# Four banks for the branch tiles, two weight differences made earlier and a residual loaded later, at the end of a two-block fp32 kernel

## What is computed

```python
merged = (jax.nn.sigmoid(m_a + b_merge[l, 0]) * (o_a @ w_branch_mla[l])
          + jax.nn.sigmoid(m_b + b_merge[l, 1]) * (o_b @ w_branch_dsa[l]))
x = x + merged @ w_out[l]
```

## Time and profile before

| | |
|---|---|
| median of 3 runs | 1223.42 us (1223.24 to 1223.59) |
| the profiled execution, whole | 1223.16 us |
| its span, first to last instruction | 1221.4 us |
| TensorE busy (matmuls) | 1208.3 us, 99% of the span |
| VectorE busy | 810.6 us, 66% |
| ScalarE busy | 645.6 us, 53% |
| HBM read and written | 109 GB/s over the span |

### The profile page before, as it was taken

One profiled execution on the slowest core, in us unless ns is written; L12 is line 12 of the kernel. 1 busy time (PEld: TensorE's weight loads), 2 busy tenths in 40 slices (PEclk: granted clock), 3 DMA queues, 4 the chain that ended last, 5 costly groups with the idle time before them and its releaser, 6 DMA issues.

```text
span 1221.4 us, 15497 instructions
## 1 busy us (share of the span) xinstructions
PE 1208.3 (99%) x5796; PEld 984.7 (81%) x5796; DVE 810.6 (66%) x1244; ACT 645.6 (53%) x930; POOL 72.8 (6%) x149
## 2 busy tenths in 40 slices
PE   8999999999999999999999999999999999999998
PEld 7888888888888888888888888888877777777876
DVE  7736543783565366559378475598679989656798
ACT  7645544663554463544444362465566555566732
POOL 2101110210111021000000000000000000000000
PEclk9999999999999999999999999999999999999999
DMA  6421322323132235313215224115213333635711
GB/s 214 136 88 36 112 69 77 103 77 103 43 112 69 78 104 203 127 35 130 112 35 189 86 65 176 35 52 207 78 60 122 118 128 109 227 119 181 276 35 69
DMA packets 25623, 134.22 MB, mean 110 GB/s; under 512 B 3352, under 2 KB 3528, under 8 KB 12768
## 3 DMA queue, kind: packets, MB, share of 16 engines
q1 hardware_dynamic: 16224, 107.14, 25.5%
q0 software_dynamic: 4736, 16.90, 4.0%
q10 hardware_dynamic: 4608, 9.44, 2.0%
HBM read 121.92 MB, written 11.55 MB: 109 GB/s over the span
## 4 chain that ended last, share of the span: by engine, by line
PE 89%; DVE 8%; issue 1%; ACT 1%; DMA 0%; ACTq 0%; DVEq 0%
PE proj L327 60%; PE proj L2015 7%; PE pm L2015 3%; PE pa L2015 3%; PE pm L1920 2%; PE pa L1931 1%; PE pa L2210 1%; PE pa L1892 1%; DVE w_lo L300 1%; PE pm L1902 1%; DVE idx L1568 1%; PE proj L1941 1%; PE pa L1941 1%; PE proj L2253 1%; PE pa L2190 1%
## 5 line engine op out<-in xcount | busy, mean ns | idle before, releaser
L327 PE MATMUL proj<-h_hi,w_hi 128*128 128x512 f32 (+1 forms) x840 | 328.7, 391 | 0.0
L327 PE MATMUL proj<-h_hi,w_lo 128*128 128x512 f32 (+1 forms) x840 | 323.9, 386 | 0.0
L327 PE MATMUL proj<-h_lo,w_hi 128*128 128x512 f32 (+1 forms) x840 | 323.6, 385 | 0.0
L300 DVE TENSOR_TENSOR w_lo<-w_raw,w_hi 128x2048 fp32r<-128x2048 f32 x80 | 182.5, 2289 | 51.7 <-ACT w_hi L294 51.3
L294 ACT ACTIVATE w_hi<-w_raw 128x2048 fp32r<-128x2048 f32 x80 | 152.4, 1913 | 68.6 <-PE proj L2015 44.2
L327 PEld LDWEIGHTS proj<-h_hi,w_hi 128*128 128x128 f32 x840 | 157.8, 188 | 35.6 <-issue 5.0
L327 PEld LDWEIGHTS proj<-h_hi,w_lo 128*128 128x128 f32 x840 | 157.8, 188 | 31.9
L327 PEld LDWEIGHTS proj<-h_lo,w_hi 128*128 128x128 f32 x840 | 158.0, 188 | 31.3 <-issue 1.0
L327 PE MATMUL proj<-w_hi,h_hi 128*128 128x512 f32 (+1 forms) x224 | 87.8, 392 | 0.4 <-issue 0.4
L327 PE MATMUL proj<-w_hi,h_lo 128*128 128x512 f32 (+1 forms) x224 | 86.8, 387 | 0.0
L327 PE MATMUL proj<-w_lo,h_hi 128*128 128x512 f32 (+1 forms) x224 | 86.7, 387 | 0.0
(11 more groups left out here) (499 smaller groups left out, 2244.2 us busy)
## 6 DMA issues: line engine op xcount, KB each, us to landing
w_raw<-in_wall SPq DMA_DIRECT2D x91, 1024.0 KB, 5.1
b<-in_wall SPq DMA_DIRECT2D x9, 1024.0 KB, 7.0
gates<-gate_st ACTq DMA_DIRECT2D x24, 256.0 KB, 2.0
m_all<-gates POOLq DMA_DIRECT2D x2, 1280.0 KB, 6.8
x_res<-in_x ACTq DMA_DIRECT2D x4, 512.0 KB, 4.9
bc<-gate_rows POOLq DMA_DIRECT2D x8, 256.0 KB, 3.5
x_res<-in_x POOLq DMA_DIRECT2D x4, 512.0 KB, 4.4
x<-x_res POOLq DMA_DIRECT2D x2, 1024.0 KB, 4.5
```

What stands on the lines that cost most here:

```text
L300: nc.vector.tensor_tensor(w_lo[:, slot, 4 * half:4 * half + 4, :], w_raw[:, half], w_hi[:, slot, 4 * half:4 * half + 4, :], ALU.subtract)\
L327: mm = nc.tensor.matmul(proj[:, bank, 0:cols] if tokens else proj[:, bank, toks], lhsT, rhs, start=(k == 0 and q == 0), stop=(k == kts - 1 ...
```

## The change

The branch tiles go in turn to four banks instead of two: `proj[:, 0]`, `proj[:, 1]`, and the two banks of `FIN_W`. Tile j waits for the product of tile j - 4 instead of j - 2. The third product of the last projection, which writes `FIN_W`, now waits for the product of tile 15, a wait that stood ahead of the fifth. The two weight differences are made ahead of the products of tiles 6 and 7 instead of 9 and 11; the first goes to a new buffer `f_three`, which lies where `f_hi`'s slots 2 and 3 are, so ScalarE waits for its low part before it writes slot 2. The two low parts of weights stand one tile earlier. POOL loads the residual only when `b12` and `b21` have landed.

```diff
+        f_three = at("f_three", -24 * K, [P, 4, 512])
...
+        BRANCH = (proj[:, 0], proj[:, 1], RES[2], RES[3])
...
             if not first:
-                nc.tensor.wait_ge(S["tile_free"], n - 1)
+                nc.tensor.wait_ge(S["tile_free"], n - 1 if free is None else free)
+            out = proj[:, bank] if out is None else out
...
             gp.wait_ge(S["o_sb"], 8)
+            gp.wait_ge(S["b12_landed"], 16 * CHUNKS + 16)
+            gp.wait_ge(S["w_landed1"], 16 * G_FIN)
             gp.dma_start(x_fin[:, :, :], x2_d.rearrange("(t p) d -> p t d", p=P)).then_inc(S["x2_landed"], 16)
...
-            fin_weight(1, 1, w_sum[:, 1, 4:8])
+            fin_weight(1, 1, f_three[:, :, :])
...
             a.wait_ge(S["merged"], 8)
+            a.wait_ge(S["d_lo"], 7 * CHUNKS + 2)
             fin_operand(2, f12)
...
             for j in range(2 * KT):
                 n = T_BR + j
-                if j == KT + 1:
+                if j == 6:
                     v.wait_ge(S["w_landed1"], 16 * G_FIN)
                     v.wait_ge(S["b12_landed"], 16 * CHUNKS + 16)
-                    v.tensor_tensor(w_sum[:, 1, 4:8], b21, b12[:, :, :], ALU.subtract).then_inc(S["t_made"], 1)
-                if j == KT + 3:
-                    fin_weight(1, 0, b11, 1)
+                    v.tensor_tensor(f_three[:, :, :], b21, b12[:, :, :], ALU.subtract).then_inc(S["t_made"], 1)
+                if j == 7:
+                    v.wait_ge(S["w_landed0"], 16 * G_FIN)
                     v.wait_ge(S["t_made"], 4 * CHUNKS + 1)
                     v.tensor_tensor(b12[:, :, :], b12[:, :, :], b11, ALU.subtract).then_inc(S["t_made"], 1)
-                if j == KT + 5:
-                    fin_weight(1, 1, w_sum[:, 1, 4:8], 2)
+                if j == KT + 2:
+                    fin_weight(1, 0, b11, 1)
+                if j == KT + 4:
+                    fin_weight(1, 1, f_three[:, :, :], 2)
                 v.wait_ge(S["tile_free"], n)
                 v.wait_ge(S["tile_made"], n + 1)
                 v.wait_ge(S["m_sig"], j + 1)
-                v.tensor_tensor(m_all[:, j], proj[:, j % 2], m_all[:, j], ALU.mult).then_inc(S["tile_free"], 1)
+                v.tensor_tensor(m_all[:, j], BRANCH[j % 4], m_all[:, j], ALU.mult).then_inc(S["tile_free"], 1)
...
-                    made(project(G_BR + kind, (1 + kind) % 2, n, j % 2, j % 4, kts=4, k0=4 * (j // 4),
+                    made(project(G_BR + kind, (1 + kind) % 2, n, None, j % 4, kts=4, k0=4 * (j // 4),
+                                 free=T_BR + max(j % 4 - 1 if kind == 0 and j < 2 else 0, 8 * kind + j - 3),
+                                 out=BRANCH[j % 4],
...
+            t_.wait_ge(S["tile_free"], T_BR + 16)
             fin_product(3, 0, 0, 2, FIN_W)
             t_.wait_ge(S["x_drained"], 8 + 2)
             fin_product(4, 0, 1, 3, FIN_X, start=False)
-            t_.wait_ge(S["tile_free"], T_BR + 16)
             fin_product(5, 1, 0, 0, FIN_Z)
```

More of the change, by code:

```diff
@@ L304, in project @@
         def project(g, slot, n, bank, j, tokens=False, act=None, kts=KT, k0=0, first=False, ready=None,
-                    last=None, cols=512, toks=slice(0, SEQ)):
+                    last=None, cols=512, toks=slice(0, SEQ), free=None, out=None):
             a_hi, a_lo = act or (h_hi, h_lo)
             if not first:
-                nc.tensor.wait_ge(S["tile_free"], n - 1)
+                nc.tensor.wait_ge(S["tile_free"], n - 1 if free is None else free)
+            out = proj[:, bank] if out is None else out
             c = slice(j * P, (j + 1) * P)
@@ L326, in project @@
                         lhsT, rhs = w[:, slot, k0 + k, c], a[:, k, toks]
-                    mm = nc.tensor.matmul(proj[:, bank, 0:cols] if tokens else proj[:, bank, toks], lhsT, rhs, start=(k == 0 and q == 0),
+                    mm = nc.tensor.matmul(out[:, 0:cols] if tokens else out[:, toks], lhsT, rhs, start=(k == 0 and q == 0),
                                           stop=(k == kts - 1 and q == 2))
```

## The result

The changed kernel takes 1226.86 us (median of 10 runs, 1225.62 to 1227.33), the kernel before beside it 1223.47 (10 runs, 1223.07 to 1223.97). The ratio is 1.0025, 95% interval 1.0015 to 1.0035: slower by 3.1 us by the ratio and by 3.4 between the medians. The forecast was 1224.9, slower by 1.5 and so within the 0.2% (75%), in a range of 1222.4 to 1226.7. The sign was right, but the loss is twice what was forecast. Its middle value, 0.25%, lies just beyond the 0.2%, which the interval still takes in. The time stands at the upper edge of the range: 1226.5 by the ratio on the 1223.42 of before, and 1226.86 as the median, 0.2 above it. The profiled execution took 1226.95 us.

What follows compares the result with a forecast made beforehand. TensorE, busy in 1208.3 of 1221.4 us, was taken as the bound, with VectorE full beside tiles 13 to 15. Removed waits gave 3.2 us, the stall cost 4.5; the end moved 1.5, to 1224.9 us, range 1222.4 to 1226.7.

Steps and rivals of the forecast that it cites:

- The two waits for banks go: TensorE's waits before tiles 13 and 15 vanish with four banks; 3.2 us if nothing else comes up.
- Low parts 6 and 7 behind the differences stall tile 8: On TensorE, tile 8 waits 1.6 us for low part 6, then 2.6 for low part 7; stall 4.5 us.
- The landing at 1153.0 without the residual: The last weights' second column lands at 1153.0 us, bounds 1152 to 1154, for 1154.7 before.
- The rival of loads that start sooner: Without the residual queued, q1 may start at 1139 and the load land at 1150.9: 1222.8 us; chance 12%.
- From the product of tile 11 to that of tile 15, 11.10 us, and 17.50 to the fourth product: VectorE's spans from tile 11 to 15, and on to the last projection's fourth product, keep their lengths.
- The sum, 1224.9: The product of tile 15 and the fourth product start 1.5 us late; 1223.42 + 1.5 = 1224.9 us.
- The mechanism stood among the rivals with 3%: TensorE's clock falls in tile 8's stall; one tile at half clock gives 1227.6 us; chance 3%.
- the rival of the late landing: The weights' load lands at 1153.95 or later, as late as 1154.7 before: up to 1226.6 us; chance 17%.

Runs made afterwards that it cites:

- experiment 3: The kernel before with the rotation over four banks alone; differences, low parts and residual stay where they were: 1224.91 us, ratio 1.0014.
- experiment 8: The kernel before with four banks alone, plus 17 unused matmuls in the wait before the last projection's fourth product: 1223.25 us, ratio 0.9999.
- experiment 1: The changed kernel with low parts 6 and 7 made right after the product of tile 5, ahead of the weight differences: 1220.25 us, ratio 0.9974.
- experiment 5: The changed kernel with both weight differences behind low part 7, ahead of the product of tile 8: 1222.87 us, ratio 0.9994.
- experiment 2: The changed kernel with the residual's load issued where it was before, right behind the gates: 1228.64 us, ratio 1.0042.
- experiment 9: The changed kernel with low parts 6 and 7 ahead of the differences and the residual's load where it was before: 1223.96 us, ratio 1.0003.
- experiment 4: The changed kernel with 15 unused matmuls added in the two waits inside tile 8: 1224.25 us, ratio 1.0007.
- experiment 7: The kernel of experiment 1 with the last projection's difference f_four made behind the low part that the fourth product waits for: 1219.33 us, ratio 0.9968.
- experiment 10: The kernel before with low parts 6 and 7 made right after the product of tile 5, nothing else changed: 1223.31 us, ratio 1.0000.
- experiment 6: The changed kernel with low parts 6 and 7 ahead of the differences, but two banks as before: 1222.80 us, ratio 0.9998.

## Why the steps were right, and the time short

*The two waits for banks go.* They did. But the 3.2 us put on them were only the seam of TensorE; the third and eighth experiments show that by themselves they are worth nothing, as the product of tile 15 is set by VectorE. The prediction's sum did not rest on them being paid, but on both engines.

*Low parts 6 and 7 behind the differences stall tile 8.* Right, and shown by the first and fifth experiments, which each remove the stall in another way. Counted from the matmul's turn to its start, as in the forecast, the waits were 1.3 (1155.11 to 1156.44) and 2.6 us (1157.23 to 1159.84) where 1.6 and 2.6 were forecast; the rows count only the idle time, 1.17 and 2.44.

*The landing at 1153.0 without the residual.* 1152.84, or 1152.63 in the time of the kernel before. The second and ninth experiments show that it would otherwise be 2.0 to 2.3 us later. The rival of loads that start sooner fell: q1 waited its 4 us again. The Trainium skill's round robin between queues (DMA: Bandwidth & Descriptors, Queues, rings and completion order) holds in this trace from 1142.4 to 1148.7, where q1 had 228 packets (1.74 MB) and q0 246 (0.95 MB), and not in the 4 us before. What holds q1 back stays open. The residual itself landed 8.4 us after its issue at 1153.42 and not in some 6; the first addition to it is at 1193.11, so this costs nothing.

*From the product of tile 11 to that of tile 15, 11.10 us, and 17.50 to the fourth product.* 11.05 (1171.54 to 1182.59) and 17.48.

*The sum, 1224.9.* Here it failed, and the step is the restart after the stall: "With slow first matmuls (0.50 for 0.39 at 1168.42) these last three take 0.82 us, so tile 9 starts at 1160.77". The matmuls came back at the full clock in the sum and at half of it on the chip, for the first 12 of 15, and the 15 took 6.00 us for 3.54. The mechanism stood among the rivals with 3%, and a price of 2.7 us for one tile that was about right (2.46 in the profile, 2.2 to 2.6 between the kernels): 12 matmuls had the slow clock, and their spacing was 1.9 and not 2 times the full one's. Its chance was too low. The forecast's own terms would have made 1224.6 with the measured start of the first difference (1152.68 in the time of the kernel before, for 1153.0), and the kernel with the stall filled took 1224.25. The mistake was to take the waits of 1.5 us at a clock of 1.00 as speaking for waits of nearly four. That the time still fell at the edge of the range was luck: the rival of the late landing had stretched it that far, and that did not come true.

## What to carry to other kernels

Before moving work to where its engine idles, list what stands behind it on that engine and who needs it by when; here two subtractions of 0.68 us, the second with a slack of 0.5, decided the sign, and putting them first made the same change pay. An engine's removed waits are worth nothing while another engine sets the end: four banks alone gave nothing with the clock held, and 2.5 us once the differences stood early. A stall of TensorE has to be priced twice when it is longer than any that the profile shows at full clock: several short waits are cheaper than one long one of the same sum, and matmuls into a free bank that fill it can be worth their while.

## What the runs showed of the hardware that was not expected

The granted clock goes with the longest wait of TensorE at this end of the kernel. The mean clock is known for every single run, so the runs with a fall can be counted; the waits are those of the profiled runs.

| longest wait in the profile | kernel | runs with a mean clock below 1 |
|---|---|---|
| 1.5 us at most | before; experiments 1, 4, 7, 8, 10 | none |
| 2.07 us | experiment 6 | 2 of 11, by 1.4 us or more above the median |
| 2.53 us | experiment 5 | 8 of 11, slower by 1.3 |
| 3.47 us | experiment 9 | 9 of 11, slower by 1.4 or more |
| 4.42 us | experiment 3 | 11 of 11 |
| 1.17 and 2.44 us, three matmuls between | the changed kernel | 10 of 10 |
| 3.25 and 2.44 us, three matmuls between | experiment 2 | 5 of 5 |

The waits stand at different places and were not varied by themselves, so the table shows a trend and no threshold. All 10 runs of the changed kernel have a mean clock below 1 (0.997 in six of them, at 1226.77 to 1227.33; 0.999 in four, at 1225.62 to 1226.27), so the same stall costs 1.3 us more in some runs than in others; the profiled run, with its 2.46 us, is one of the six. The Trainium skill (TensorE: Matmul & The Clock Gate, Part 1) says that the moment at which the clock changes is run-variable, since the activity is looked at on a schedule that does not start with the kernel. The two groups are in keeping with it, but no run here shows that schedule. In the third experiment the clock fell only after TensorE had resumed: three matmuls at the full pace, then eight or nine at half. In the fifth and ninth it fell likewise, behind five or six matmuls. In the changed kernel it had fallen before the matmuls came back.
